# Splitting peer_v ahead of time, and alternating two token blocks on PE, in an encoder layer's expert stage

## What is computed

```python
    s = jnp.einsum('thpc,hpkc->thpk', qh, peer_keys)          # 8 heads, 2 x 128 keys
    s_top, i_top = lax.top_k(s, PEER_TOPK)                    # 16 of each
    ...
    best, pos = lax.top_k(cand, PEER_TOPK)                    # 16 experts a head
    g = jax.nn.softmax(best, axis=-1)                         # 128 experts a token in all
    u = peer_u[idx]
    a = jax.nn.gelu(jnp.einsum('td,ted->te', xb, u), approximate=False)
    w = (g * a)
    return jnp.einsum('te,ted->td', w, peer_v[idx])
```

## Time and profile before

| what | value |
|---|---|
| median of 3 runs | 4344.81 us (4338.82 to 4346.47) |
| the profiled execution | 4337.67 us, its span 4335.7 us |
| PE busy | 3612.2 us (83%) |
| DVE busy | 3183.3 us (73%) |
| ACT busy | 1302.0 us (30%) |
| POOL busy | 939.4 us (22%) |
| moved by DMA | 856.46 MB, mean 198 GB/s |
| first matmul of experts, last `use` | 2073.3, 4279.96 us |

### The profile page before, as it was taken

The page is one execution under the profiler, slowest core; times in us unless marked ns, Lnnn a source line. Parts: engine busy times, 40 slices in busy tenths (PEclk is TensorE's granted clock), DMA queues, the critical chain, the costliest instruction groups (busy, mean ns, idle before and its releaser), DMA issues. The chain is left out here.

```text
span 4335.7 us, 59165 instructions
## 1 busy us (share of the span) xinstructions
PE 3612.2 (83%) x19538; PEld 1998.8 (46%) x19538; DVE 3183.3 (73%) x5656; ACT 1302.0 (30%) x2576; POOL 939.4 (22%) x1038
## 2 busy tenths in 40 slices
PE   6956468899689757487899999999999999999993
PEld 3535344455345423366345454544444454454442
DVE  1024431222459978899699999999899999999998
ACT  2131222211223233344233332333333333332331
POOL 0000000000000000000344444444443444444444
PEclk9966569999899878655899999999999999999996
DMA  2100020210211010266788888889888888888885
GB/s 92 63 26 1 0 84 29 99 38 0 84 61 38 22 62 0 79 194 193 293 337 328 340 330 327 331 323 341 314 329 326 326 334 324 341 325 319 334 329 184
DMA packets 238936, 856.46 MB, mean 198 GB/s; under 512 B 16080, under 2 KB 119312, under 8 KB 167440
## 3 DMA queue, kind: packets, MB, share of 16 engines
q0 software_dynamic: 73728, 536.90, 32.7%
q1 hardware_dynamic: 165136, 318.63, 21.2%
HBM read 792.55 MB, written 62.91 MB: 197 GB/s over the span
## 5 line engine op out<-in xcount | busy, mean ns | idle before, releaser
L1579 POOL COPY x_index<-expert 128x1 uint32 (+1 forms) x512 | 333.9, 652 | 2951.2 <-POOLq L1379 2068.0
L70 PE MATMUL x_ps_v<-x_v_hi,x_w_hi 128*128 128x512 f16 x1536 | 604.6, 394 | 134.4 <-DVE x_w_lo L1683 77.5
L1582 POOL DMA_INDIRECT x_rows<-in_peer_uv,x_index x512 | 581.9, 1137 | 406.9 <-POOL x_index L1579 393.1
L1653 DVE SCALAR_TENSOR_TENSOR acc<-x_rows,x_share,acc 128x1024 f32<-128x1024 f32 x512 | 654.8, 1279 | 0.0
L1737 PE MATMUL x_ps_a<-h_hi,x_u_hi 128*128 128x256 f16 (+1 forms) x2048 | 620.5, 327 | 18.4 <-ACT x_u_hi L1595 15.8
L1738 PE MATMUL x_ps_a<-h_lo,x_u_hi 128*128 128x256 f16 (+1 forms) x2048 | 620.2, 327 | 0.0
L71 PE MATMUL x_ps_v<-x_v_lo,x_w_hi 128*128 128x512 f16 x1536 | 603.8, 393 | 0.0
L72 PE MATMUL x_ps_v<-x_v_hi,x_w_lo 128*128 128x512 f16 x1536 | 602.3, 392 | 0.0
L1606 ACT ACTIVATE x_dots<-x_dots 128x1 f32<-128x1 f32 x512 | 103.9, 203 | 1328.4 <-DVE x_dots L1671 1328.4
L1671 DVE CUSTOM_DVE_ANT_0 x_rows<-h_lo,x_rows 128x1024 f32<-128x1024 f32 x256 | 312.4, 1220 | 124.5 <-DMA x_rows<-in_peer_uv,x_index 123.5
L1742 PE MATMUL x_ps_a<-h_hi,x_u_lo 128*128 128x256 f16 (+1 forms) x2048 | 374.6, 326 | 0.0
(11 more groups left out here) (286 smaller groups left out, 6398.2 us busy)
## 6 DMA issues: line engine op xcount, KB each, us to landing
x_u_st<-in_peer_u_t SPq DMA_DIRECT2D x128, 512.0 KB, 5.9
x_v_st<-in_peer_v SPq DMA_DIRECT2D x128, 512.0 KB, 5.8
gate_scratch<-g_out SPq DMA_DIRECT2D x24, 2048.0 KB, 8.7
x_gate<-gate_scratch SPq DMA_DIRECT2D x32, 1024.0 KB, 8.7
x_gate<-gate_scratch SPq DMA_DIRECT2D x32, 512.0 KB, 3.7
m_w_st<-in_w_merge SPq DMA_DIRECT2D x8, 1536.0 KB, 6.4
k_w_st<-in_w_route SPq DMA_DIRECT2D x16, 576.0 KB, 3.7
x_rows<-in_peer_uv,x_index POOLq DMA_INDIRECT x512, 6.9
```

What stands on the lines that cost most here:

```text
L70: pe.matmul(out, lhs_hi, rhs_hi, start=first, stop=False)
L1579: pool.tensor_copy(index[:, m % RING:m % RING + 1], R.expert[:, tile, bass.ds(hk, 1)]).then_inc(index_ok, 1)
L1582: pool.indirect_dma_start(rows[:, m % RING], None, uv_all, bass.IndirectOffsetOnAxis(ap=index[:, m % RING:m % RING + 1], axis=0)).then_inc ...
L1653: dve.scalar_tensor_tensor(R.acc[:, DT + tile], rows[:, r, D:2 * D], share[:, s:s + 1], R.acc[:, DT + tile], ALU.mult, ALU.add).then_inc(v ...
```

## The change

1. **v is split ahead of time.** A new class `Ahead` takes 512 KB tiles of `peer_v`: POOL loads one into one of two slots, ACT makes the high half, DVE the low half, POOL stores both halves (512 KB) to a DRAM scratch `v_scratch`. 40 tiles are treated in `project` (one behind each of the ten v tiles, three a column tile in ten of the 13 column tiles), 88 in `merge` (4, 4 and 3 behind a column tile's blocks, half of them ahead of `m_hi`). In `experts` SP loads the halves, two groups' worth of buffers; ACT and DVE split no v there.
2. **PE's order in experts** is now: large A of group i, small V of group i-1, small A of group i, large V of group i. Two groups make one turn of the loop. The visits are laid out anew.
3. **Gates**: SP loads them in three pieces of 256 tokens into a staging buffer, ACT copies each into a table [expert, token], so that DVE reads it without a stride. Gelu writes straight into `w`, the gate product is made in place, with two slots for both.
4. **Index**: POOL copies four index columns at once, one copy for four visits.
5. **Semaphores** are freed behind each of eight stages: a clear and one more all-engine barrier.

```diff
+V_EARLY = 40
+V_TILE = 11
+class Ahead:
...
+    def load(self, pool, A, n, s, first=False):
+        if not first:
+            pool.wait_ge(self.v_lo_ok, n - 1)
+        pool.dma_start(self.st[:, s], A["peer_v"][n + self.first]).then_inc(self.v_in[s], 16)
+
+    def high(self, act, n, s, nth, first=False):
+        act.wait_ge(self.v_in[s], 16 * nth)
+        if not first:
+            act.wait_ge(self.v_out[s], 16 * nth - 16)
+        act.activation(self.out[:, s, 0], self.st[:, s], ACT.Copy, scale=VSCALE).then_inc(self.v_hi_ok, 1)
+
+    def low(self, dve, n, s):
+        dve.wait_ge(self.v_hi_ok, n + 1)
+        dve.scalar_tensor_tensor(self.out[:, s, 1], self.st[:, s], VSCALE, self.out[:, s, 0], ALU.mult,
+                                 ALU.subtract).then_inc(self.v_lo_ok, 1)
+
+    def store(self, pool, n, s):
+        pool.wait_ge(self.v_lo_ok, n + 1)
+        pool.dma_start(self.R.v_dram[n + self.first], self.out[:, s]).then_inc(self.v_out[s], 16)
+
+    def moves(self, pool, A, count):
+        self.load(pool, A, 0, 0, True)
+        self.load(pool, A, 1, 1, True)
+        with pool.Fori(0, count // 2 - 1) as i:
+            for s in range(2):
+                self.store(pool, 2 * i + s, s)
+                self.load(pool, A, 2 * i + (2 + s), s)
...
 def project(nc, A, R):
...
+                    if turn is not None:
+                        ahead.high(act, TT + 6 * turn + (at + b), (at + b) % 2, 3 * turn + (TT // 2 + (at + b) // 2 + 1))
...
+    def release(self):
+
+        self.nc.clear_and_free_semaphores(self.stage)
+        self.stage = []
+        self.nc.all_engine_barrier()
...
 def merge(nc, A, R):
...
+        ahead = Ahead(nc, c, R, "m", V_EARLY)
+        SHARE = (4, 4, 3)
...
+                    early, late = units(i, q, b)
+                    for v, slot, nth in early:
+                        ahead.high(act, v, slot, nth, isinstance(v, int) and v < 2)
                     wait_apart(act, mg_ok, n + 1)
                     act.activation(R.m_hi[:, m, t0:t0 + n_t], mg[:, s, 0:n_t], ACT.Copy).then_inc(mg_hi, 1)
+                    for v, slot, nth in late:
+                        ahead.high(act, v, slot, nth)
...
 def experts(nc, A, R):
...
+        AT = {("l", 0): 1, ("l", 1): 1, ("l", 2): 2, ("l", 3): 1,
+              ("vs", 0): 2, ("vs", 1): 1,
+              ("s", 0): 1, ("s", 1): 1, ("s", 2): 1, ("s", 3): 0,
+              ("vl", 0): 1, ("vl", 1): 1, ("vl", 2): 2, ("vl", 3): 1}
...
+            def group(i, slot, _nth, first, last):
+                if last:
+                    return
+                load_gates(i + 1, 0, 3 * i + 3)
+                load_u(i + 1, 0)
+                load_u(i + 1, 1)
+                load_gates(i + 1, 1, 3 * i + 4)
+                load_v(i + 1, 1 - slot, 0, first)
+                load_v(i + 1, 1 - slot, 1, first)
+                load_u(i + 1, 2)
+                load_gates(i + 1, 2, 3 * i + 5)
+                load_v(i + 1, 1 - slot, 2, first)
+                load_u(i + 1, 3)
+                load_v(i + 1, 1 - slot, 3, first)
...
+                    if m % PER_TILE == 0:
+                        pool.tensor_copy(index[:, tile % 2], R.expert[:, tile, bass.ds(hk, PER_TILE)]).then_inc(index_ok, 1)
+                        wait_apart(pool, index_ok, GT * i + tile + 1)
...
+            def gates(n, piece, taken):
+
+                t0, _ = PIECES[piece]
+                act.wait_ge(gate_in, 16 * n + 16 * (piece + 1))
+                if taken is not None:
+                    act.wait_ge(w_ok, taken)
+                act.activation(gate[:, :, t0:t0 + PIECE], gate_st[:].rearrange("p t e -> p e t"),
+                               ACT.Copy).then_inc(gate_ok, 1)
...
+                def gelu(k, n_t):
+                    act.wait_ge(a_mm, A_STEPS * i + k + 1)
+                    if not first or k >= SLOTS_G:
+                        act.wait_ge(w_lo_ok, A_STEPS * i + k - SLOTS_G + 1)
+                    act.activation(w[:, k % SLOTS_G, 0:n_t], ps_a[:, k % 4, 0:n_t], ACT.Gelu,
+                                   scale=1 / WSCALE).then_inc(gelu_ok, 1)
...
+                if not first:
+                    add(V_STEPS * (i - 1) + TL - 1, (TL - 1) % 2, TL - 1)
+                dve.wait_ge(gate_ok, 3 * i + 2)
+                for e in range(E):
+                    gated(e, LARGE)
+                    if e:
+                        low(e - 1, LARGE)
+                    visits(("l", e))
+                low(E - 1, LARGE)
+                for t in range(TS):
+                    visits(("vs", t))
+                    if not first:
+                        add(V_STEPS * (i - 1) + TL + t, t % 2, TL + t)
...
+                for t in range(TL):
+                    visits(("vl", t))
+                    if not last:
+                        u_low(i + 1, t)
+                    if t < TL - 1:
+                        add(V_STEPS * i + t, t % 2, t)
...
+            def group(i, slot, nth, first, last):
+                a_block(i, 0, LARGE, first)
+                if not first:
+                    small(i - 1, 1 - slot)
+                a_block(i, E, SMALL, first)
+                pe.wait_ge(w_lo_ok, A_STEPS * i + E)
+                pe.wait_ge(v_in[slot], 16 * E * nth + 16 * E)
+                v_block(i, slot, 0, LARGE, first)
```

More of the change, by code:

```diff
@@ L674, in merge, with _, units @@
             "w_hi_ok w_lo_ok mm sig prod mg_ok mg_hi mg_lo".split()]
+        ahead = Ahead(nc, c, R, "m", V_EARLY)
+        SHARE = (4, 4, 3)
+        assert sum(SHARE) == V_TILE
         block = c.enter_context(nc.Block())
+        @block.gpsimd
+        def _(pool):
+            ahead.moves(pool, A, KO * V_TILE)
+        def units(i, q, b):
+            off = sum(SHARE[:b]) - q * V_TILE
+            each = [(2 * V_TILE * i + (off + r), (off + r) % 2, V_TILE * i + ((off + r) // 2 + 1)) for r in range(SHARE[b])]
+            return each[:2], each[2:]
         @block.sync
@@ L739, in steps @@
                     dve.tensor_tensor(mg[:, s, 0:n_t], t1[:, 0:n_t], t2[:, 0:n_t], ALU.add).then_inc(mg_ok, 1)
+                    early, late = units(i, q, b)
+                    for v, slot, nth in early:
+                        ahead.low(dve, v, slot)
                     dve.wait_ge(mg_hi, n + 1)
@@ L1636, in group @@
-                high(n, k % 2, *before)
-                for t in range(DT):
-                    if t < E and not last:
-                        u_split(i + 1, t)
-                    visits(("v", t))
-            for e in range(E):
-                u_split(0, e, True)
-            group(0, True)
-            with act.Fori(1, N_GROUPS - 1) as i:
-                group(i, False)
-            group(N_GROUPS - 1, False, True)
+                def gelu(k, n_t):
[4 more added lines that the diff above has]
+                                   scale=1 / WSCALE).then_inc(gelu_ok, 1)
@@ L1704, in group @@
-                low(n, k % 2, *before)
-                for t in range(DT):
-                    dve.wait_ge(v_mm, V_STEPS * i + t + 1)
-                    dve.scalar_tensor_tensor(R.acc[:, t], ps_v[:, t % 2], 1 / (VSCALE * GSCALE), R.acc[:, t],
-                                             ALU.mult, ALU.add).then_inc(added, 1)
-                    visits(("v", t))
-                    if t < E and not last:
-                        u_split(i + 1, t)
-            for e in range(E):
-                u_split(0, e, True)
@@ new lines, in group @@
+                dve.wait_ge(gate_ok, 3 * i + 3)
+                for e in range(E):
+                    gated(E + e, SMALL)
+                    if e:
+                        low(E + e - 1, SMALL)
+                    visits(("s", e))
+                low(2 * E - 1, SMALL)
+                for t in range(TL):
+                    visits(("vl", t))
+                    if not last:
+                        u_low(i + 1, t)
+                    if t < TL - 1:
+                        add(V_STEPS * i + t, t % 2, t)
@@ L1765, in _, with a_block @@
-            group(0, True)
-            with pe.Fori(1, N_GROUPS) as i:
-                group(i, False)
+            def a_block(i, k0, part, first):
+                t0, n_t = part
+                t = slice(t0, t0 + n_t)
+                for e in range(E):
+                    k = k0 + e
+                    out = ps_a[:, k % 4, 0:n_t]
+                    if not first or k >= 4:
+                        pe.wait_ge(gelu_ok, A_STEPS * i + k - 3)
+                    if k < E:
+                        pe.wait_ge(u_hi_ok, E * i + e + 1)
+                    for ko in range(KO):
+                        pe.matmul(out, u_hi[:, e, ko], R.h_hi[:, ko, t], start=ko == 0, stop=False)
+                        pe.matmul(out, u_hi[:, e, ko], R.h_lo[:, ko, t], start=False, stop=False)
+                    if k < E:
+                        pe.wait_ge(u_lo_ok, E * i + e + 1)
+                    for ko in range(KO):
+                        last = pe.matmul(out, u_lo[:, e, ko], R.h_hi[:, ko, t], start=False, stop=ko == KO - 1)
```

(15 more changed lines are left out.)

328 lines of the change are left out of this document (166 added, 162 removed).

## The result

| | before | after |
|---|---|---|
| median | 4345.18 us (8 runs) | 4362.59 us (8 runs, 4354.21 to 4375.81) |
| ratio | | 1.0043, 95% interval 1.0029 to 1.0058 |
| profiled execution | 4337.67 us | 4366.44 us |

The change makes the kernel **slower by 0.4%**. Where the time went is read from the stages. A stage ends where the barrier behind it passes; the expert stage is counted from ScalarE's first split of u to its first instruction in the final norm, and its period from the first Gelu of group 1 to that of group 31.

What follows compares the result with a forecast made beforehand. DVE and its row fetches were taken to set the expert stage's period. Profiled 4337.7 us - 170 (experts) + 71 (merge) + 3 (first loads) + 4 (clears) = 4246; median 4253, rounded to 4250, range 4175 to 4340.

Steps and rivals of the forecast that it cites:

- the forecast's small terms for first loads and clears: First v loads ahead of x loads in projection and merge, 3 us; eight semaphore clears with second barriers, 4 us.
- The slots' turn-round: Merge: one turn of a v-split slot takes 7.8 us, so the units set the pace, costing 71 us.
- the prediction's 792.7: Merge: the time in us at which the v-split units begin, behind the first sigmoid.
- The 3 us a tile for the weight splits: Merge: some 3 us added per tile where its own weight split stands in the queues.
- So PE does not wait, with 1.8 us to spare: Expert stage: PE's 62.3 us list is the longer, and DVE's adds come in time, by a 1.8 us margin.
- 0.7 us a group: Expert stage: loss charged for late row fetches, giving a period of 63.0 us, 170 us saved in all.
- brings it back in step: Expert stage: DVE's 5.7 us of waiting for Gelus in large A lets it realign with PE.
- Projection, "0": Projection: three units in 13.0 us allow a slot turn of 8.7 us, so the v split costs nothing there.
- 3 for the first loads of both stages: Projection and merge: the first two v loads go ahead of the x loads, costing 3 us.
- the slots' turn-round eats the gain: Rival, chance 0.13: merge waits for POOL's loads with a slot turn of 10.4 us, against 170 saved; 4386 us.
- rows become the bound: Rival, chance 0.12: expert rows landing near 9 us make PE wait 3.7 us a group, period 66; 4349 us.
- The two signs of being wrong: POOL's copies landing under 3.5 or over 6 us; DVE waiting for rows above 4 us a group in experts.

Runs made afterwards that it cites:

- Three slots: Kernel after with three slots instead of two for the v split in merge (loop written out, two buffers overwritten in place): 4266.7 us, 0.983 of before.
- load first: Kernel after with POOL issuing the next unit's load ahead of the present unit's store: 4377.2 us.
- moved visit: Kernel with three slots, one of a group's 16 sparse visits moved from small A to the first place in large A: 4194.6 us.
- X stores early: Kernel with three slots and the moved visit, x's two DRAM stores issued behind projection's first weight load instead of at its end: 4185.7 us, 0.964 of before.
- Gates later: Kernel with three slots, ScalarE copying the first group's third gate piece behind the large block's products, not ahead of the first Gelu: 4278.8 us.

## Why the prediction was wrong

The forecast was 4246 us for the profiled execution's own time, and 4366 came; the median, 4362.6, lies above the range. The 120 us, by the prediction's steps (they sum to 124, as the forecast's small terms for first loads and clears are not taken off everywhere):

- **"The slots' turn-round", R = 7.8: mis-sized, 44 us.** The mechanism was right: ScalarE waits for the loads, PE for mg, and the barrier passes late. But from the load's issue to its split went 5.00 us where I had 4.25 (4.1 from rows, and 0.15 for the store ahead of it from none), the hand-overs took 0.72 (0.69 of them to POOL) where I had 0.3, from no row either, and only the store's issue was quicker, 0.61 for 0.96: 8.62. 44 x 0.82 are 36 us; POOL's drain behind the last store, which no term held, is 5.4 more; and the first unit's split came some 3 us later than the prediction's 792.7 (819.3 here, where the stage begins 23.5 us later). The 3 us a tile for the weight splits were about right: 26 us instead of 24. Three slots show the slots to be the cause; load first and the packets show that the load waits behind the store, which the prediction weighed only in its slower rival.
- **"So PE does not wait, with 1.8 us to spare": the failing step, 54 us** (32 x (64.7 - 63.0); by the mark of the earlier trace rows, 64.5, it is 48, and the ends named below are 11 instead of 5). Both lists of work were right: PE's came out at 62.3 us in the run with the moved visit, to the tenth, and DVE's, the period less its waits for rows and Gelu (64.7 - 237.3/32), at 57.3 where I had 56.3. The margin was wrong. I charged the fetch with 0.7 us a group as an average; rows in fact came late just before the one add that PE needs first, where, as I read it, v's loads are in flight. DVE waited 110.3/32 = 3.4 us a group for rows, and its idle time in large A, which "brings it back in step", comes after the add, not before it.
- **Projection, "0" and 3 for the first loads of both stages: a failing step, some 11 us.** I had compared R with the time between units and left the stores of x out, which the trace of before shows as well (issued at 207.96 and 208.34): work moved into a stretch whose other traffic I had not listed. X stores early shows it: with the stores moved the projection ends at 259.2.
- **The first group** cost PE 17.7 us ahead of its first add, which no term held; with the last group's end it leaves the experts 5 us short beyond the period. Gates later shows that waiting for the third gate copy is not the cause; the cause stays open.
- **Attention and fourier**, +10 us, don't follow from the change: 493.7 to 498 us in eleven of the fourteen later runs, whatever their edit, 503 to 506 in the other three. In these three and in after PE was busy for 310 to 312 us with the same 1536 matmuls that took it 301 to 304 in the others; the granted clock between 300 and 500 us was 0.53 in the profile of after, 0.57 in that of before. Why is open.
- **Right:** PE's wait for w_lo gone but for 1.1 us, the clock near 1.00, the gate product at 0.69 and 0.42 us, the eight clears with barriers at about 0.5 us each, and the gate copies without effect on the time, although each took 2.08 us, more than either of my bounds (1.05 and 1.77).

Both slower rivals came in part: R lies between the forecast's 7.8 and the 10.4 of "the slots' turn-round eats the gain", the period between 63.0 and the 66 of "rows become the bound". By the number the second is nearest (4349), but only the first, 4386, was clearly slower than before. It was to decide at R = 9.7; with an expert gain of 111 instead of 170 its own formula gives 8.7, and with the drain and the stores of x the 8.6 measured was enough. The chances took the merge and the experts as separate risks, where each needed only to be a little off. The two signs of being wrong that I could have read as measures, loads landing over 6 us and waits for rows over 4 us a group, stayed quiet at 4.9 and 3.4.

The prediction gave two statements of the Trainium skill (DMA: Bandwidth & Descriptors). By the anatomy of a GpSimd-issued DMA a 512 KB transfer takes an estimated 3.2 us. POOL's stores in merge agree with it at a median of 3.0 us; its loads, issued behind them, don't: 4.9, never under 3.97. The share of 358 GB/s that the page gives a core does not bind here, with one core at work: a stretch of 15 us ran at 410 GB/s, and the expert stage with the moved visit at 356 GB/s as a whole, faster than the 343 of after.

## What to carry to other kernels

A stage that is "free" because DMA, ScalarE and VectorE have room is not free if its work goes through two slots in order: write the turn out hop by hop, with every hand-over and with the load behind the store where one queue carries both, and give it the slots that the turn asks for. Where two engines' lists are near each other, look at which single item the one waits for first, and place flexible work where the other idles and transfers are few; one visit of 2.3 us moved was worth 71 us. Count what other queues send in the stretch into which work is moved.

## What was unexpected of the hardware

- In merge, with DMAs issued by POOL, POOL's closing drain took 5.4 us after the last transfer had landed (5.6 with three slots), in projection 6.6. In the kernel before, where POOL does nothing in merge, it took 34 ns.
- Of a load and a store of 512 KB issued by POOL 0.6 us apart, the one issued second lands about 5 us after its issue, whichever it is, the first in 3.0 (store) or 4.4 (load); in the turn of after shown its first packet starts 0.3 us after the last one of the first transfer.
- ScalarE's copy of 1024 values a partition with a stride of four elements took 2.08 us, a contiguous one 1.05.
